# A hybrid decoder kernel: attention products in pairs, the attention norm behind the recurrence, and constant products on TensorE

## What is computed

```
A  sparse attention, 6 heads of 64, one shared key and value head:
   score[q,s] = sum over 8 index heads of relu(iq_h . ik) * iw_h      (causal)
   the 256 best keys of each query are kept; softmax over them; times v
   o_a = o_a * rsqrt(mean(o_a^2) + eps) * attn_norm_g                 (over 384 features)
B  RWKV-7: per head a 64 x 64 state with a data-dependent decay and a delta rule over 1024
   steps, then a group norm, a bonus term and a gate                  (384 features)
C  causal pooling over 2, 4, 8 and 16 tokens                          (256 features)
mix = concat(o_a, o_b, o_c) @ w_out
x = LN(ALPHA * x + mix);  x = LN(ALPHA * x + squared-ReLU MLP + gated embedding)
```

## Time and profile before

| | before |
|---|---|
| median of three runs | 3678.16 us |
| the profiled execution | 3676.48 us, of which its span is 3674.7 us |
| TensorE (PE) busy | 3361.9 us, 91% |
| VectorE (DVE) busy | 1912.7 us, 52% |
| ScalarE (ACT) busy | 1066.6 us, 29% |
| GpSimd (POOL) busy | 1179.9 us, 32% |
| mean granted TensorE clock | 0.961 of full speed |
| chain that ended last | PE 60%, DVE 13%, issue 11%, DVEq 9% |

### The profile page before, as it was taken

The page is one execution under the profiler, slowest core; times in us unless marked ns, Lnnn a source line. Parts: engine busy times, 40 slices in busy tenths (PEclk is TensorE's granted clock), DMA queues, the critical chain, the costliest instruction groups (busy, mean ns, idle before and its releaser), DMA issues.

```text
span 3674.7 us, 61308 instructions
## 1 busy us (share of the span) xinstructions
PE 3361.9 (91%) x23032; PEld 2436.3 (66%) x23032; DVE 1912.7 (52%) x3091; ACT 1066.6 (29%) x1873; POOL 1179.9 (32%) x972
## 2 busy tenths in 40 slices
PE   7888987998999999999988889879889999999997
PEld 3444444885677888888734444558765788888884
DVE  5688996444442333333348989754346133333335
ACT  3334234443122121121134342444422122121222
POOL 1266542651211222222123754245412122222221
PEclk9999998998999999999999999989999999999998
DMA  3100000000101111111111000000011111111111
GB/s 120 42 28 17 26 20 19 1 0 18 63 12 61 48 46 51 46 46 49 42 45 38 25 17 26 14 19 0 1 35 58 35 46 46 51 46 51 46 46 46
DMA packets 43861, 132.70 MB, mean 36 GB/s; under 512 B 9280, under 2 KB 11840, under 8 KB 43072
## 3 DMA queue, kind: packets, MB, share of 16 engines
q1 hardware_dynamic: 37280, 122.41, 10.3%
q10 hardware_dynamic: 6432, 8.40, 0.8%
HBM read 117.15 MB, written 5.24 MB: 33 GB/s over the span
## 4 chain that ended last, share of the span: by engine, by line
PE 60%; DVE 13%; issue 11%; DVEq 9%; ACT 2%; POOLq 2%; POOL 1%; ACTq 1%; DMA 1%; SPq 0%
PE bank L1053 14%; PE bank L1054 14%; PE bank L1055 14%; DVE M L1677 7%; DVEq L1681 7%; PE bank L777 3%; PE bank L655 2%; PE wide L620 2%; DVE PB L1693 2%; PE wide L777 2%; PE bank L745 1%; POOLq L1553 1%; ACTq L406 1%; DVE WK L1679 1%; PE bank L704 1%
## 5 line engine op out<-in xcount | busy, mean ns | idle before, releaser
L1552 POOL TENSOR_TENSOR WL<-WR,WH 128x1024 fp32r<-128x1024 f32 x160 | 402.7, 2517 | 1485.8 <-ACT WH L1343 1485.1
L1053 PE MATMUL bank<-XH,WH 128*128 128x512 f32 x1280 | 517.8, 405 | 18.3 <-POOLq L1553 9.5
L655 PE MATMUL bank<-X,WR 128*128 128x512 f32 (+1 forms) x1088 | 515.3, 621 | 10.6 <-ACT X L1110 9.3
L1055 PE MATMUL bank<-XH,WL 128*128 128x512 f32 x1280 | 502.6, 393 | 0.0
L1054 PE MATMUL bank<-XL,WH 128*128 128x512 f32 x1280 | 502.4, 392 | 0.0
L1053 PE MATMUL bank<-HH,WH 128*128 128x512 f32 x1024 | 400.4, 391 | 0.0
L1054 PE MATMUL bank<-HL,WH 128*128 128x512 f32 x1024 | 398.8, 389 | 0.0
L1055 PE MATMUL bank<-HH,WL 128*128 128x512 f32 x1024 | 398.5, 389 | 0.0
L1343 ACT ACTIVATE WH<-WR 128x1024 fp32r<-128x1024 f32 x160 | 168.3, 1053 | 737.3 <-PE bank L1055 728.7
L655 PEld LDWEIGHTS bank<-X,WR 128*128 128x128 f32 x1088 | 206.7, 199 | 262.3 <-issue 237.9
L1937 DVE TENSOR_TENSOR RB<-RB 128x512 f32<-128x512 f32 x128 | 88.6, 692 | 547.8 <-ACT RB L1369 547.8
(11 more groups left out here) (280 smaller groups left out, 5234.6 us busy)
## 6 DMA issues: line engine op xcount, KB each, us to landing
WR<-in_w SPq DMA_DIRECT2D x128, 512.0 KB, 3.5
WR<-in_w_in SPq DMA_DIRECT2D x34, 512.0 KB, 3.5
WR<-in_w_out SPq DMA_DIRECT2D x16, 512.0 KB, 3.6
WR<-in_w_gate SPq DMA_DIRECT2D x16, 512.0 KB, 6.2
Y<-in_xT SPq DMA_DIRECT2D x2, 2048.0 KB, 13.0
out_T<-X SPq DMA_DIRECT2D x1, 4096.0 KB, 11.1
QZS<-QZ ACTq DMA_DIRECT2D x48, 64.0 KB, 2.0
QZS<-QZ ACTq DMA_DIRECT2D x64, 48.0 KB, 1.9
```

What stands on the lines that cost most here:

```text
L655: mm = e.matmul(BK_[hf][:, 0:q.stop - q.start], WR[:, i % RING, kt, :], X[:, kt, q], start=kt == 0, stop=kt == KT - 1)
L1053: e.matmul(BK_[b], WH[:, s, w, :], high[:, kt, q], start=kt == 0, stop=False)
L1055: mm = e.matmul(BK_[b], WL[:, s, w, :], high[:, kt, q], start=False, stop=kt == kts - 1)
L1552: e.tensor_tensor(WL[:, s, :, :], WR[:, i % RING, :, :], WH[:, s, :, :].bitcast(F32), ALU.subtract)
```

## The change

**Products with values in pairs.** The words `pv.b.1`, `.3` and `.5` are gone. `pv.b.h` waits for both heads h and h + 1 and issues their products alternately: key tile 0 of head h, key tile 0 of head h + 1, key tile 1 of head h, and so on.

**First selected block's scores on VectorE.** For block 3, ScalarE only takes the relu, and VectorE itself multiplies by the weight and adds (`first_scores`, 8 operations on 512 columns and the causal add). GpSimd's `lg.3` words and ScalarE's scalings of that block are gone.

**The norm.** The `norm` words are gone. There is one `sqrt` of all 1024 columns at the end of the list. `cp.0` and `cp.1` copy `O2` over the keys. The reciprocal of 1024 columns (`inverse_rms`) comes after the second meeting, ahead of VectorE's first mask; the three products of 1024 columns (`scale_attention`) come in the post-processing, behind `bonus(0)`. `RSD` moves to memory that outlives stage 1.

**The key products.** VectorE does all three; `keys_normed` is gone.

**Constant products.** `keep_clock(bank, n)` issues n products of the identity and 512 constant columns into a bank that is free there, and nothing reads them: five behind the second meeting, one at each of three places of the last tile where the other tiles issue the next tile's products, and four behind the last `gate`, ahead of the third meeting.

**New lists.** All four lists are written anew. TensorE's projection quarters come earlier relative to the attention words, and none is left among the words of blocks 7 and 2 at the end; the key norms `n.0`, `n.1` come before `pt.7.0` where they were among `s.2` and at the very end. In the first lines, `round.3` comes seven times before `qc.0`; before, `qc.0` and `q.0` came first.

```
 VECTOR_ORDER (its head and its end)
-    z.0.0 iqc.3 iq.3 vt.0 qc.0 q.0 round.3*2 s.0.0 s.0.1 z.0.1 round.3*4 s.0.2 s.0.3 round.3*6 s.0.4 s.0.5 qc.1 q.1
...
-    qc.2 q.2 inv.7 fin.7 s.2.0 s.2.1 s.2.2 s.2.3 norm.4 norm.0 s.2.4 norm.7 s.2.5 norm.5 inv.2 norm.3 fin.2 norm.6
-    norm.1 norm.2
+    z.0.0 iqc.3 iq.3 vt.0 lg.3.0 lg.3.1 lg.3.2 lg.3.3 lg.3.4 lg.3.5 lg.3.6 lg.3.7 round.3*7 qc.0 round.3 q.0 round.3
...
+    s.7.1 round.2*7 s.7.2 s.7.3 round.2*4 bias.2 s.7.4 s.7.5 qc.2 q.2 inv.7 fin.7 s.2.0 s.2.1 s.2.2 s.2.3 s.2.4
+    s.2.5 cp.0 inv.2 fin.2 cp.1
 TENSOR_ORDER (its head and its end)
-    z.0.0*4 c.3 z.3.0 iq.3 z.3.0*3 lg.3.0 vt.0 z.1.0*3 lg.3.1 z.1.0 lg.3.2 lg.3.3 z.2.0*2 lg.3.4 z.2.0 lg.3.5 z.2.0
...
-    pv.7.2 pv.7.3 s.7.4 s.7.5 z.16.0 pt.7.4 pt.7.5 fin.7 pv.7.4 pv.7.5 s.2.0 s.2.1 z.16.1 pt.2.0 pt.2.1 ss.7 s.2.2
-    pv.2.0 pv.2.1 s.2.3 z.16.1*2 pt.2.2 pt.2.3 s.2.4 pv.2.2 pv.2.3 s.2.5 n.0 pt.2.4 z.16.1 pv.2.4 pt.2.5 pv.2.5
-    fin.2 ss.2 n.1
+    z.0.0*4 c.3 z.3.0 iq.3 z.3.0*3 lg.3.0 lg.3.1 vt.0 z.1.0 lg.3.2 lg.3.3 z.1.0 lg.3.4 lg.3.5 z.1.0 lg.3.6 lg.3.7
+    z.1.0 z.2.0*4 z.0.1 q.0 z.0.1*3 s.0.0 s.0.1 q.1 pt.0.0 z.1.1 pt.0.1 z.1.1 s.0.2 s.0.3 pv.0.0 z.1.1 pt.0.2 pt.0.3
...
+    z.16.1 ss.6 z.16.1 n.1 pt.7.0 pt.7.1 pv.7.0 s.7.2 s.7.3 pt.7.2 pt.7.3 pv.7.2 s.7.4 s.7.5 pt.7.4 pt.7.5 fin.7
+    pv.7.4 s.2.0 s.2.1 pt.2.0 pt.2.1 ss.7 s.2.2 s.2.3 pv.2.0 pt.2.2 pt.2.3 pv.2.2 s.2.4 s.2.5 pt.2.4 pt.2.5 fin.2
+    pv.2.4 ss.2
 SCALAR_ORDER (its end)
-    s.2.3 pt.2.2 pt.2.3 s.2.4 pt.2.4 s.2.5 z.16.1 pt.2.5 fin.2 sq.2 ss.2 sqrt.1 n.0 n.1
+    ss.7 s.2.2 s.2.3 pt.2.2 pt.2.3 s.2.4 s.2.5 pt.2.4 pt.2.5 fin.2 sq.2 ss.2 sqrt.0 n.0 n.1
 POOL_ORDER (its end)
-    shift.15*6 shift.16*6
+    q.6 shift.10*2 lg.7.1 lg.7.2 lg.7.3 shift.11*6 lg.7.4 lg.7.5 shift.12*3 lg.7.6 lg.7.7 shift.12*3 q.7 shift.13*6
+    bias.6 shift.14*6 lg.2.1 lg.2.2 lg.2.3 shift.15 lg.2.4 lg.2.5 shift.15 lg.2.6 lg.2.7 shift.15*4 q.2 shift.16*6
+    bias.7
...
+            def keep_clock(bank, n):
+                for _ in range(n):
+                    e.matmul(BK_[bank], ident, C1[:, 0:HALF], start=True, stop=True)
...
-                    e.wait_ge(wide[w].free, wide[w].read(L, ("pt", b, h)))
+                    for g in range(2):
+                        e.wait_ge(wide[g].free, wide[g].read(L, ("pt", b, h + g)))
                     for kt in range(b + 1):
-                        mm = e.matmul(NARROW[0][lo:lo + HD, h // 2 * P:(h // 2 + 1) * P], VT[:, kt, 0:HD],
-                                      PT[:, w, kt, :], start=kt == 0, stop=kt == b)
-                    mm.then_inc(pv_done, 1)
+                        for g in range(2):
+                            mm = e.matmul(NARROW[0][HD * g:HD * (g + 1), h // 2 * P:(h // 2 + 1) * P], VT[:, kt, 0:HD],
+                                          PT[:, g, kt, :], start=kt == 0, stop=kt == b)
+                            if kt == b:
+                                mm.then_inc(pv_done, 1)
...
                 meet(e, L, 1)
+                keep_clock(7, 5)
...
+                post_read(e, L, ("gate", 0), 0)
+                keep_clock(2, 4)
                 meet(e, L, 2)
...
+            def first_scores(L, b, h):
+                n, to, x = (b + 1) * P, SC[:, SLOT[b], 0:(b + 1) * P], R[:, h % 2, 0:(b + 1) * P]
+                e.wait_ge(first_relu, L * IH + (h + 1))
+                settle(e)
+                if h == 0:
+                    e.drain()
+                    e.tensor_scalar(to, x, IW[:, b, h:h + 1], None, ALU.mult).then_inc(first_used, 1)
+                else:
+                    e.scalar_tensor_tensor(to, x, IW[:, b, h:h + 1], to, ALU.mult, ALU.add).then_inc(first_used, 1)
...
-                    if i < NP - 1:
-                        e.drain().then_inc(keys_normed, 1)
-                    else:
-                        e.drain()
-                        e.tensor_tensor(BZ[:, BK + i, :], BZ[:, BK + i, :], T1[:, i, :], ALU.mult)
+                    e.drain()
+                    e.tensor_tensor(BZ[:, BK + i, :], BZ[:, BK + i, :], T1[:, i, :], ALU.mult)
...
                 e.memset(PX[:, :, :, 0:1], 1.0).then_inc(px_ones, 1)
+                inverse_rms(L)
...
-                for i in range(NP):
+                bonus(0)
+                scale_attention()
+                for i in range(1, NP):
                     bonus(i)
```

More of the change, by code:

```diff
@@ L155 @@
[L155 to L158 removed]
+    z.0.0 c.3 iq.3 z.3.0 lg.3.0 lg.3.1 lg.3.2 lg.3.3 lg.3.4 lg.3.5 lg.3.6 lg.3.7 z.1.0 z.2.0 q.0 z.0.1 s.0.0 q.1
@@ L1270, in _ @@
                     elif kind == "sqrt":
-                        for q in SQRT_COLUMNS[b]:
+                        for q in (slice(0, S),):
                             e.drain()
@@ L1670, in topk_round @@
                 src = work if i or drop else SC[:, s, 0:n]
-                if i == 0:
-                    e.wait_ge(scores_ready, L * NTOP + (TOP_ORDER.index(b) + 1))
+                if i == 0 and b != TOP_ORDER[0]:
+                    e.wait_ge(scores_ready, L * (NTOP - 1) + TOP_ORDER.index(b))
                     settle(e)
@@ L1710, in finish_attention, with over_keys, inverse_rms, scale_attention @@
                 e.tensor_tensor(O2[:, q], NARROW[0][:, 2 * P:3 * P], SPR[:, 2, :], ALU.mult).then_inc(narrow.free, 1)
-            def normalise(L, b):
+            def first_scores(L, b, h):
[5 more added lines that the diff above has]
+                    e.tensor_scalar(to, x, IW[:, b, h:h + 1], None, ALU.mult).then_inc(first_used, 1)
+                else:
+                    e.scalar_tensor_tensor(to, x, IW[:, b, h:h + 1], to, ALU.mult, ALU.add).then_inc(first_used, 1)
+                e.drain()
+                if h == IH - 1:
+                    e.tensor_tensor(to[:, b * P:n], to[:, b * P:n], causal, ALU.add)
+                    e.drain()
+            def over_keys(L, part):
                 last = TOP_ORDER[-1]
+                q = [slice(0, last * P), slice((last + 1) * P, S)] if part == 0 else [slice(last * P, (last + 1) * P)]
                 e.wait_ge(par_landed, L * 16 + 16)
-                e.wait_ge(rms_ready, L * 3 + (3 if b == last else 2))
                 settle(e)
-                q = slice(b * P, (b + 1) * P)
-                e.reciprocal(RSD[:, q], RSD[:, q])
                 e.drain()
-                for p in range(3):
-                    src = O2[:, q] if p == 2 else A3[:, p, q]
-                    dst = A3[:, 2, q] if p == 2 and b >= last else src
-                    e.scalar_tensor_tensor(dst, src, par_col("ag", p), RSD[:, q], ALU.mult, ALU.mult)
-                if b == last:
-                    e.tensor_copy(A3[:, 2, 0:b * P], O2[:, 0:b * P])
+                for x in q:
+                    e.tensor_copy(A3[:, 2, x], O2[:, x])
+            def inverse_rms(L):
+                e.wait_ge(rms_ready, L + 1)
+                settle(e)
+                e.reciprocal(RSD[:, :], RSD[:, :])
+            def scale_attention():
+                for p in range(3):
+                    e.scalar_tensor_tensor(A3[:, p, :], A3[:, p, :], par_col("ag", p), RSD[:, :], ALU.mult, ALU.mult)
             def full(T, bank, use):
@@ L1817, in _ @@
                         finish_attention(L, b)
-                    elif kind == "norm":
-                        normalise(L, b)
+                    elif kind == "lg":
+                        first_scores(L, b, h)
+                    elif kind == "cp":
+                        if b == 0:
+                            e.wait_ge(wide[1].full, wide[1].written(L, ("s", TOP_ORDER[-1], NH - 1)))
+                            settle(e)
+                        over_keys(L, b)
                 meet(e, L, 0)
```

114 lines of the change are left out of this document (59 added, 55 removed).

## The result

| | before | after |
|---|---|---|
| median of the runs, us | 3680.57 (4 runs, 3670.18 to 3683.76) | 3620.55 (4 runs, 3615.08 to 3624.32) |
| ratio | 1 | 0.9841, 95% interval 0.9826 to 0.9857 |
| profiled execution / its span, us | 3676.48 / 3674.7 | 3620.73 / 3618.7 |
| TensorE busy, us | 3361.9 | 3279.5 |
| mean granted TensorE clock | 0.961 | 0.962 |

A forecast was written before the change was run, and what follows sets the result against it. VectorE was taken to bound attention from its first selection round to the mask of block 2. Per layer 26.6 + 1.8 + 3.0 - 0.7 - 0.75 = 29.95 us, 59.9 for two, from 3676.5 to 3617 us; range 3602 to 3648.

The forecast's parts named there:

- The start: First selection round on VectorE at 95.9 us instead of 113.66, 17.8 us earlier; net 14.7 us per layer.
- The stretch behind it: First selection round to mask of block 2: 7.1 us per layer given back, with 4 us slippage at five hand-overs.
- VectorE standing for over 10 us: Sign that the forecast is wrong: VectorE idle that long between 96 and 545 us, in attention.
- rival (a): Attention's lists: VectorE starts 18 us earlier but stands later; 18 us slippage, a layer gains 16, 3645 us; chance 0.14.
- The value pairs: Attention's value products alternate between two heads: 55 ns each instead of 102, freeing 20 us of TensorE time per layer.
- Rival (b): Attention's value products don't overlap, 102 ns stay and the moved work isn't paid for: 9 us per layer, 3635; chance 0.07.
- The end of attention: Mask of block 2 to preparation: 12.5 us saved up to the last value product, 3.4 behind it, per layer.
- The key products: Preparation, all on VectorE: scans no longer held up by GpSimd; 1.8 us saved per layer, with a short wait gone.
- The reciprocal: 1024 columns on VectorE ahead of its first mask: 6.55 us within idle time, costs nothing, 2.2 us to spare.
- rival (c): Long reciprocal locks GpSimd out; its products ahead of the recurrence start up to 6.5 us later per layer: 3630; chance 0.07.
- The constant products: Per layer: 3.0 us gained at the recurrence's start through TensorE's clock; 0.7 lost in the last tile, 0.75 behind the gate.
- Rival (d): Attention's five hand-overs fail each time: over 6.0 us late at each loses the gain, 9 us gives 3707; chance 0.04.

The follow-up runs named there:

- run with the start alone: Kernel before, with only the first selected block's logits in pairs and their weighting and sum on VectorE; 3657.5 us, ratio 0.9948.
- the warm run: Changed kernel plus constant products (36, 6, 2, 1, 1) in TensorE's idle times around the end of attention, to hold its clock full; 3627.09 us, ratio 0.9865.

## Why the prediction was right, and where it was not

3617 us was forecast and 3620.55 measured, on the side that was likeliest and for mostly the reasons given. That the two lie so close is in part luck. The stages of the sum gained 52.5 us in the profiled executions where 59.9 were forecast; 3.5 more came from dense parts outside of the sum, and the kernel before was 4 us slower by its median than the execution that the forecast started from.

**The start** was right to 0.2 us in layer 0 and 0.5 in layer 1. **The stretch behind it** was right in sum: 7.1 us were to be given back, 7.9 and 9.1 were. The parts were not. The wait of 1.8 us at the second rotation of block 0 did not come (it ran at 109.17 with no idle time before it), and the 12.7 us of waits lie at one hand-over. By the prediction's own test, "VectorE standing for over 10 us", rival (a) was at work there, at less than half of its price of 18 us. The run with the start alone gave back 9.3 and 9.6 us without the pairs and most of the new lists, so giving back belongs at least in part to the early start itself.

**The value pairs** overlap: 55 ns were taken, 1.97 us for 32 is 62 with the last one's latency. Rival (b) is out. That TensorE's freed time pays for the moved work is not borne out: with heads one after the other and the work moved all the same, the stretch lost only 2 to 3 us, and the end 5.5. TensorE had room for most of it anyway.

**The end of attention** is the step that failed: "12.5 us saved" and 3.4 behind it. 10.4 and 10.3 came. The last part held (last value product at 581.3, 5.8 us to the preparation, forecast 6.6), so that in layer 0 it gave 4.2 and the chain before it 6.2 of the 12.5. That chain was built with durations of a busy TensorE, 1.7 us for a pair and 0.6 for transpositions; with the moved work gone TensorE was at half clock and took 3.4 to 3.7. That is 2.7 us by the layers that differ in the second pair alone, 1.5 and 3.3 by the warm run. The rest is the list: value products ahead of the logits that VectorE waits for, and the finish of block 7 ahead of block 2's logits on VectorE. Three pairs of block 2 were forecast at 4.5 us each and took 5.5, 6.4 and 5.6. Moving those words gave 5 and then another 2 to 4 us per layer, more than was missing, though half of the first 5 is the clock again. What the moved projection and key norms, and the norm's move, each give in the end, no run undid alone.

**The key products:** 1.8 forecast, 2.5 and 2.3 measured, and 2.7 and 3.0 in the run that undid them. From the first scan to the third it takes 13.41 us before and 13.36 after, where the sum had after 0.4 us *longer* (2.46 of products against 1.8 and 0.3); the third scan gives 2.16, and the way from its end to the recurrence 0.3. By the Trainium skill (SBUF — State Buffer, section "SBUF: two separate sides") a VectorE operation with two SBUF inputs and a GpSimd one that reads SBUF lock each other out for a whole instruction. The trace agrees: with GpSimd's product back, the third scan ends 2.15 us behind that product's end, and alone it takes 2.28.

**The reciprocal:** 6.55 us to the digit; rival (c) is out, GpSimd ran on. The three products were said to be hidden "even if GpSimd holds VectorE up for 2 us": they took 1.7 us more beside GpSimd and were hidden.

**The constant products.** Behind the second meeting 3.0 was forecast; 3.6 and 0.4 came against before. Over the 20 layers that ran with five, the way to the second tile was 27.1 to 30.5 us, 28.9 on average, and 31.3 and 31.6 without: 2.5 us. The ten of them whose first two masks lie 1.06 us apart (full clock) took 27.8 on average, the ten with 1.77 (half clock) 30.0. The last tile: 0.7 forecast, 0.7 and 0.8 against the run without. The gate: 0.75 forecast, 0.6 measured, no gain, as said. What wasn't forecast is that the last tile became 1.3 and 2.0 us shorter all the same. The longest row of it in the kernel before is a stand of TensorE in the middle of a line's products, for nothing that the trace names:

```profile
838.88 0.50 PE L860 MATMUL wide<-AM,WU 64*64 64x64 f32 x18 [2.02 <-issue]
```

Four such stands add up to 5.5 us there (1.49, 1.00, 0.99, 2.02) and to some 1.5 us after. The instructions are the same but for the constants. That they are waits for instructions was not tried; it stays open.

**Rival (d)** needed over 6.0 us at each of five hand-overs; it had 12.7 at one. Slower was never near.

## What to carry to other kernels

Work that fills idle time in a latency chain may also hold TensorE's clock: before it is moved away, redo the chain with durations at the lower clock. In a strict list, put what the bounding engine waits for (logits) ahead of what nobody waits for (value products, finishes); that brought more here than filling the idle time with constant products did, in part because the clock came back with it. And products of 64-column stationaries that write alternate halves of the partitions overlap: 1.97 instead of 3.30 us for 32.

## What the runs showed that was not expected

- A warm end did not make a faster kernel: 1.5 to 3.3 us per layer won in the end, and the ratio to before was 0.9865 against 0.9841. Some of it was lost where the recurrence then began at half clock, some in the last tile; why, no run tells.
- Stages that no edit touched differ by several us between layers and executions: the end 33.7, 36.3 or 39.5 us with the clock, the first tile 27.1 to 30.5 us in part with it. One execution can't judge a kernel to 3 us; stage lengths can, where the clock is the same.
- The last tile took 28.2 to 33.9 us in kernels whose instructions in it hardly differ; what sets it stays open.
